# Suffix sums of the stick-breaking attention by plain fp32 products, in place of a high and a low part

## The reference, cut to what matters

```
z = jnp.einsum('bhqd,bshd->bhqs', qblk, kf) * (dh ** -0.5)
causal = kpos[None, :] < qpos[:, None]
sp = jnp.where(causal, jax.nn.softplus(z), 0.0)
after = lax.cumsum(sp, axis=3, reverse=True) - sp
a = jnp.where(causal, jnp.exp(jax.nn.log_sigmoid(z) - after), 0.0)
return jnp.einsum('bhqs,bshd->bqhd', a, vf)
```

## Time and profile before

| | |
|---|---|
| time, median of 3 runs | 2325.12 us (2322.39 to 2327.33) |
| profiled execution | 2326.91 us |
| its span in the trace | 2325.0 us |
| TensorE busy | 2256.1 us (97%) |
| VectorE busy | 1330.6 us (57%) |
| ScalarE busy | 1085.5 us (47%) |
| mean transfer rate | 173 GB/s |

### The profile page before, as it was taken

The page is one execution under the profiler, slowest core; times in us unless marked ns, Lnnn a source line. Parts: engine busy times, 40 slices in busy tenths (PEclk is TensorE's granted clock), DMA queues, the critical chain, the costliest instruction groups (busy, mean ns, idle before and its releaser), DMA issues.

```text
span 2325.0 us, 27182 instructions
## 1 busy us (share of the span) xinstructions
PE 2256.1 (97%) x11140; PEld 1863.6 (80%) x11140; DVE 1330.6 (57%) x1658; ACT 1085.5 (47%) x1340; POOL 18.1 (1%) x53
## 2 busy tenths in 40 slices
PE   8999899999999899999999989999999999899999
PEld 6888778887888678888888878778888888778887
DVE  5455465456545764556447756655456456456455
ACT  5444555445444554445444444545445444455443
POOL 0000000000000000000000000000000000000000
PEclk9999999999999899999999999999999999999999
DMA  8555337654654456547555534436556655336553
GB/s 290 184 173 180 107 105 226 195 186 164 215 190 130 142 172 199 186 136 241 185 180 172 181 109 145 145 114 213 192 174 200 203 183 162 122 121 206 180 181 114
DMA packets 212940, 401.50 MB, mean 173 GB/s; under 512 B 12368, under 2 KB 30928, under 8 KB 212688
## 3 DMA queue, kind: packets, MB, share of 16 engines
q1 hardware_dynamic: 212816, 399.76, 53.3%
HBM read 398.66 MB, written 1.05 MB: 172 GB/s over the span
## 4 chain that ended last, share of the span: by engine, by line
PE 89%; DVE 5%; ACT 3%; issue 1%; DMA 1%; SPq 0%; POOL 0%; ACTq 0%; DVEq 0%; POOLq 0%
PE ps L1098 27%; PE ps L1100 27%; PE ps L1099 27%; PE ps L1141 5%; DVE wl L769 2%; ACT wh L496 1%; DMA raw<-in_ffn_w_in 1%; PE ps L1415 1%; PE ps L1312 0%; ACT arena L670 0%; PE ps L1331 0%; ACT arena L669 0%; DMA raw<-in_swa_w_in 0%; DVE htl L1038 0%; DVE arena L1036 0%
## 5 line engine op out<-in xcount | busy, mean ns | idle before, releaser
L769 DVE TENSOR_TENSOR wl<-raw,wh 128x1024 fp32r<-128x1024 f32 x730 | 867.6, 1222 | 577.2 <-ACT wh L496 572.9
L496 ACT ACTIVATE wh<-raw 128x1024 fp32r<-128x1024 f32 x730 | 753.4, 1058 | 578.3 <-PE ps L1100 418.8
L1098 PE MATMUL ps<-wh,xh 128*128 128x512 f32 (+1 forms) x2320 | 889.3, 383 | 4.7 <-DVE xl L776 4.7
L1099 PE MATMUL ps<-wl,xh 128*128 128x512 f32 (+1 forms) x2320 | 878.4, 379 | 0.0
L1100 PE MATMUL ps<-wh,xl 128*128 128x512 f32 (+1 forms) x2320 | 878.0, 378 | 0.0
L1098 PEld LDWEIGHTS ps<-wh,xh 128*128 128x128 f32 x2320 | 439.5, 189 | 86.9 <-DVE xl L776 6.4
L1100 PEld LDWEIGHTS ps<-wh,xl 128*128 128x128 f32 x2320 | 439.1, 189 | 82.1
L1099 PEld LDWEIGHTS ps<-wl,xh 128*128 128x128 f32 x2320 | 439.7, 190 | 77.5
L1098 PE MATMUL ps<-wh,hth 128*128 128x512 f32 x736 | 289.4, 393 | 1.4 <-DVE htl L782 1.4
L1100 PE MATMUL ps<-wh,htl 128*128 128x512 f32 x736 | 286.8, 390 | 0.0
L1099 PE MATMUL ps<-wl,hth 128*128 128x512 f32 x736 | 286.6, 389 | 0.0
(11 more groups left out here) (103 smaller groups left out, 924.2 us busy)
## 6 DMA issues: line engine op xcount, KB each, us to landing
raw<-in_ffn_w_in SPq DMA_DIRECT2D x352, 512.0 KB, 4.6
raw<-in_ffn_w_out SPq DMA_DIRECT2D x176, 512.0 KB, 4.4
raw<-in_dil_w_in SPq DMA_DIRECT2D x72, 512.0 KB, 4.0
raw<-in_sb_w_in SPq DMA_DIRECT2D x48, 512.0 KB, 4.3
raw<-in_ple_w_gate SPq DMA_DIRECT2D x32, 512.0 KB, 4.8
raw<-in_sb_w_out SPq DMA_DIRECT2D x16, 512.0 KB, 4.2
gb<-in_ln_g SPq DMA_DIRECT2D x12, 512.0 KB, 3.7
gb<-in_ln_b SPq DMA_DIRECT2D x12, 512.0 KB, 5.1
```

The costliest lines, as they stand in the source:

```text
L496: act.activation(wh[:, u % RING, :], raw[:, u % RAWS, :], ACT.Copy).then_inc(hi_done, 1)
L769: dve.tensor_tensor(wl[:, u % RING, :], raw[:, u % RAWS, :], wh[:, u % RING, :].bitcast(F32), ALU.subtract).then_inc(lo_done, 1)
L1098: pe.matmul(out_, a_h, b_h, start=start, stop=False)
L1099: pe.matmul(out_, a_h, b_l, start=False, stop=False)
```

## The change

`soft` makes only `ssp` and raises `sp_done` with it. `cum` takes `ssp` itself, in plain fp32, against the fp32 constants: four products instead of eight, now in the order 384, 128, 384, 128 columns. The fp32r copies of the two matrices, and the two copies on ScalarE that made them, are gone. Every other order stays.

```diff
-        lower_r = sb("lower_r", [P, P], F32R)
-        ones_r = sb("ones_r", [P, P], F32R)
...
-                    act.activation(lower_r[:], const("lower"), ACT.Copy).then_inc(masks_done, 1)
-                    act.activation(ones_r[:], const("ones"), ACT.Copy).then_inc(masks_done, 1)
...
-                    own(dve.scalar_tensor_tensor(ssp[:, h % 2], zpair(h), 0.0, sw[:, h % 2], ALU.max, ALU.add))
-                    own(dve.tensor_copy(sph[:, h % 2], ssp[:, h % 2]))
-                    dve.tensor_tensor(spl[:, h % 2], ssp[:, h % 2], sph[:, h % 2].bitcast(F32), ALU.subtract).then_inc(sp_done.sem, 1)
+                    dve.scalar_tensor_tensor(ssp[:, h % 2], zpair(h), 0.0, sw[:, h % 2], ALU.max, ALU.add).then_inc(sp_done.sem, 1)
...
                 def cum(hh, h):
                     pe.wait_ge(sp_done.sem, sp_done.at(i, hh, h))
                     for m in range(2):
-                        for of in (sph, spl):
-                            pe.matmul(zpair(h)[:, m, :], lower_r[:], of[:, h % 2, m, :], start=False, stop=False, skip_group_check=True)
-                    for m in range(2):
-                        for of in (sph, spl):
-                            ins = pe.matmul(zpair(h)[:, m, P:2 * P], ones_r[:], of[:, h % 2, m, 2 * P:3 * P], start=False,
-                                            stop=of is spl, skip_group_check=True)
+                        pe.matmul(zpair(h)[:, m, :], const("lower"), ssp[:, h % 2, m, :], start=False, stop=False, skip_group_check=True)
+                        ins = pe.matmul(zpair(h)[:, m, P:2 * P], const("ones"), ssp[:, h % 2, m, 2 * P:3 * P], start=False,
+                                        stop=True, skip_group_check=True)
                     ins.then_inc(cum_done.sem, 1)
...
-                    pe.wait_ge(masks_done, 4)
+                    pe.wait_ge(masks_done, 2)
```

More of the change, by code:

```diff
@@ L176, in build_program @@
         sa = pair_buffer(vv)
-        sph, spl = (v.rearrange("p c t m -> p (c t m)").rearrange("p (b h n) -> p b h n", b=2, h=2) for v in (hth, htl))
         ps = ctx.enter_context(nc.psum_tensor("ps", [P, 8, BLK], F32))
```

## The result

| | before | after |
|---|---|---|
| median | 2325.91 us (4 runs, 2322.39 to 2327.33) | 2307.81 us (4 runs, 2307.5 to 2308.28) |
| span of the profiled execution | 2325.0 | 2305.6 |
| ratio, after to before | | 0.9925, 95% interval 0.9907 to 0.9942 |

The kernel became faster by 0.75%; 2308 was forecast. The runs of after also lie closer together: 0.8 us apart against 4.9.

What follows compares the result with a forecast made beforehand. TensorE, 89% of the chain of waits, bounds the kernel; four halves shrink from 91.65 to 74.3 us, 17.3 saved (5.0 arithmetic, 12.4 half-speed clock), from the median 2325.12 to 2308, range 2302 to 2317.

Steps and rivals of the forecast that it cites:

- The removed passes: In soft on VectorE, cast and subtraction go, so sp_done rises 1.58 us earlier, on the path twice in each half.
- cum in plain fp32: On TensorE, four plain fp32 products take 1.83 us after a wait against 1.19, 0.64 more per cum on the path.
- lower bound: For cum's price: if sharing the array halves a pass's speed, one alone takes 0.16 and 0.11 us; cum stays 1.19.
- doubled pass: Slower rival: a pass over all rows and columns takes twice as long, cum 3.5 us, total 2331; 5%.
- four loads: Rival: each 128-column fp32 product is four passes, each held by a load; cum 2.27 us, total 2313; 7%.
- The sum: All-warm stages from cum(0) to av(2): halves of 18.31 and 18.85 us, four together 74.3 instead of 91.65, 17.3 saved.
- 12.4 us of slow clock: Part of the 17.3 us saved in the four halves: the half-speed clock that TensorE's waits bring; arithmetic gives 5.0.
- The clock falls as before: Rival: shorter waits ahead of cum, same fall; 1.7 us saved, 2323. Wholly 6%; in part, 2313 to 2320, 13%.
- the wait ahead of 248.81: TensorE's wait before cum(1) in the first half; called one of the shorter, though its four products took 1.65 us.
- fp32 is dearer: Rival on cum's full-array products: four loads, 2313, 7%; on the slower side, double passes, 2331, 5%.
- More than forecast: Rival: clock falls elsewhere may drop, or a pass be as cheap as the lower bound; 2300 to 2303, 10%.
- the wait for q's tokens: TensorE's wait at the end of a first half; claimed to stay, hanging on cum(3), weights(3), splits and L901, all unchanged.

## Why the prediction was right

**The removed passes.** 1.58 us off sp_done, twice a half: the first-half start of cum(1) was forecast at 2.20 behind cum(0), and the rows show 2.15 (244.09 to 246.24). From av(1) to cum(2) 5.81 was forecast, and 5.80 stand there (250.27 to 256.07). The two runs that put the passes ahead of and behind the signal show that only the place counts.

**cum in plain fp32.** Forecast 1.72 for its passes, 1.83 behind a wait. Measured passes 0.32 and 0.11, as taken; 1.76 for cum(2), and 1.93 for cum(1). Ahead of av, whose products fill half of the array's columns, the last 128-column product takes 0.31 (247.86 to 248.17), not the 0.22 of the one before; ahead of the unit's fp32r product it takes 0.14 (257.69 to 257.83). Doubling the products confirmed the 1.72 within 0.1 a cum. The lower bound (1.19), the doubled pass (3.5) and the four loads (2.27) are out.

**The sum.** 18.31 and 18.85 forecast for a half, 18.42 and 18.99 measured; 17.3 us in all, 16.9 measured in the halves. The span lost 2.5 more outside them. 0.9 us of that came before the first half: its cum(0) starts at 244.09, not 245.03. That is scatter: in after and in the same kernel with soft ahead of the splits, z(1), which comes ahead of all that differs between them, starts at 237.39 and at 239.55. Behind the first half of layer 0 (to the next cum(0)) after is 1.6 longer, behind that of layer 3 it is 1.3 shorter, and between the two layers it is 2.0 shorter. Each time the shorter trace is the one with less time at half speed: in before the clock did not fall behind the first half of layer 0, and it was slow longer than in after behind that of layer 3 and between the layers. Whether the change has a part in these I can't say from one trace of each.

That 2308 was met to 0.2 is in part luck. The forecast took 17.3 us off a median of 2325.12; the runs beside the result gave 2325.91 for before, so 18.1 went. And the 12.4 us of slow clock were read from one execution of before, while its executions lie up to 15.5 us apart.

**The clock.** The 12.4 us that the sum gave to the slow clock came back whole: no half of after, nor of any run whose waits ahead of cum were 1.5 us or less, has a granted clock under 1.00. With the passes ahead of sp_done they were 1.9 to 2.5 us, and it fell in each of the four halves. That the waits bring the fall is shown by this run and the one with the passes behind the signal, which gives the engines the same work. Which waits do it I can't say: the clock fell behind six of eight in before and behind five of eight with the passes ahead. Ahead of cum(2) in the earlier trace rows, 2.46 us did not bring it down, and 1.88 us did in that run. (The wait ahead of 248.81, which the prediction calls one of the shorter, is 2.52 us, longer than four of the eight.)

**The rivals.** "The clock falls as before" is out, and so is "fp32 is dearer", in both sizes. "More than forecast" did not come about in the product's price. At the end of the first halves the clock did fall in after, behind the wait for q's tokens that the prediction left in place; moving the tokens gained 7.7 us with high and low part and 6.3 in plain fp32, more than the 5 us of idle time. With high and low part the trace without the move shows why: the clock fell behind that wait in both layers. In plain fp32 it fell in neither, so the 1.3 us over the 5 are not explained there.

What the prediction did not see: it took the order around `soft` as given. Of the 7.39 us from av(1) to cum(2), 2.28 were a unit's split, 1.05 on ScalarE and 1.23 on VectorE, that cum(2) did not need; cast and subtraction were 1.58.

## What to carry to other kernels

A pass that makes operands cheaper to multiply is worth its time while it hides; before trading it for dearer products, look at what stands ahead of it in its engine's order. Here moving soft ahead of the splits gave nearly twice what removing the passes gave (ratios to before 0.9853 and 0.9925), and made removing them a loss. A wait of TensorE is worth more than its length if the clock falls behind it, so add the slow stretch to its price; and price a longer instruction ahead of a wait as filling it.

## What the runs showed of the hardware

- A plain fp32 product over the full array was two passes with a weight load each, 0.32 us for 384 columns and 0.11 for 128. The fp32r products took 0.17 and 0.11: at 128 columns two fp32r products and one plain fp32 product (two passes) cost the same, 0.22. All of the 0.6 us a cum came from the 384-column products.
- Half-speed time varies from execution to execution, and with it the total. Before ranged over 15.5 us in 20 executions: the fastest, 2318.54 us, had a mean granted clock of 0.990, the slowest, 2334.07, one of 0.984. After ranged over 0.8 us in 4, and the doubled products, with no slow clock in the halves, over 4.5 in 10.
